# Attention heads grouped by the half in which their key/value head lies, and value products of 256 columns

## What is computed

```
q = q.reshape(bsz, nc, CHUNK, SWA_KV_HEADS, SWA_GROUP, SWA_HEAD_DIM) * SWA_HEAD_DIM ** -0.5
sc = jnp.einsum('bncvgd,bnkvd->bvgnck', q, k_band)
sc = sc + bias[None, :, :, None]
...
p = jnp.exp(sc - m)
p = p / (p.sum(-1, keepdims=True) + jnp.exp(sink - m))
o = jnp.einsum('bvgnck,bnkvd->bncvgd', p.astype(v_band.dtype), v_band)
o = o.reshape(bsz, s, SWA_WIDTH)
return (o * jax.nn.silu(gate)) @ w_out
```

## Time and profile before

| | |
|---|---|
| Median of 3 runs | 2330.74 us (2328.17 to 2332.15) |
| Profiled execution, its own time | 2325.54 us |
| Its span in the trace | 2323.7 us |
| PE busy | 2285.1 us, 98% |
| DVE, ACT, POOL busy | 75%, 50%, 15% |
| Chain that ended last | PE 78%, DVE 13%, issue 4%, DMA 3% |

### The profile page before, as it was taken

How to read it: one execution, slowest core, us unless ns; L and a number is a source line. 1 busy time by engine, 2 the same in 40 slices (tenths; PEclk the granted TensorE clock), 3 DMA queues, 4 the chain that set the end, 5 groups by cost and what they waited for, 6 DMA issues and landing times.

```text
span 2323.7 us, 30739 instructions
## 1 busy us (share of the span) xinstructions
PE 2285.1 (98%) x11554; PEld 1895.7 (82%) x11554; DVE 1753.4 (75%) x2442; ACT 1161.5 (50%) x1706; POOL 339.9 (15%) x340
## 2 busy tenths in 40 slices
PE   8999999999999999999999999999999999999997
PEld 6878878878888888887888888888888888888886
DVE  8788898875857669887696866897568667789448
ACT  4344455366435445536654544553655445554464
POOL 2311211122010111012201001110210110011031
PEclk9999999999999999999999999999999999999999
DMA  8787768654725435874484554585257345355324
GB/s 309 269 302 246 233 227 286 232 175 138 261 91 174 149 122 177 294 237 163 155 281 127 166 169 130 175 275 189 69 189 265 126 135 171 120 184 177 118 82 136
DMA packets 131043, 437.07 MB, mean 188 GB/s; under 512 B 13840, under 2 KB 18464, under 8 KB 130896
## 3 DMA queue, kind: packets, MB, share of 16 engines
q1 hardware_dynamic: 113232, 369.28, 48.4%
q0 software_dynamic: 17664, 65.83, 8.0%
HBM read 373.45 MB, written 57.41 MB: 185 GB/s over the span
## 4 chain that ended last, share of the span: by engine, by line
PE 78%; DVE 13%; issue 4%; DMA 3%; ACT 1%; POOL 1%; SPq 0%; POOLq 0%; DVEq 0%; ACTq 0%
PE accs L686 22%; PE accs L688 21%; PE accs L687 21%; DVE w_lo L1415 3%; PE bank L686 2%; PE bank L688 2%; PE bank L687 2%; PE bank L797 1%; PE bank L966 1%; PE bank L982 1%; PE bank L903 1%; PE bank L948 1%; DVE z L1759 1%; DMA stage<-w_qk 1%; DMA stage<-t_prep 1%
## 5 line engine op out<-in xcount | busy, mean ns | idle before, releaser
L1415 DVE TENSOR_TENSOR w_lo<-stage,w_hi 128x1024 fp32r<-128x1024 f32 x524 | 644.1, 1237 | 328.6 <-ACT w_hi L1057 327.5
L1057 ACT ACTIVATE w_hi<-stage 128x1024 fp32r<-128x1024 f32 x524 | 550.1, 1055 | 469.9 <-PE accs L688 179.6
L686 PE MATMUL accs<-w_hi,xs 128*128 128x512 f32 x1128 | 445.9, 395 | 7.9 <-ACT sg L1062 4.9
L688 PE MATMUL accs<-w_hi,xs 128*128 128x512 f32 x1128 | 439.8, 390 | 0.0
L687 PE MATMUL accs<-w_lo,xs 128*128 128x512 f32 x1128 | 439.3, 389 | 0.0
L686 PEld LDWEIGHTS accs<-w_hi,xs 128*128 128x128 f32 x1128 | 212.0, 188 | 54.4 <-issue 11.3
L688 PEld LDWEIGHTS accs<-w_hi,xs 128*128 128x128 f32 x1128 | 211.7, 188 | 45.0
L687 PEld LDWEIGHTS accs<-w_lo,xs 128*128 128x128 f32 x1128 | 212.0, 188 | 42.0
L686 PE MATMUL accs<-x_hi,w_hi 128*128 128x512 f32 (+1 forms) x640 | 244.2, 382 | 2.1 <-DVE qT L1860 1.5
L2134 POOL TENSOR_TENSOR rstd<-ve,half 128x1 f32<-128x1 f32 x96 | 81.6, 851 | 1124.5 <-DVE ve L1485 878.8
L688 PE MATMUL accs<-x_hi,w_lo 128*128 128x512 f32 (+1 forms) x640 | 236.5, 370 | 0.0
(11 more groups left out here) (213 smaller groups left out, 3780.9 us busy)
## 6 DMA issues: line engine op xcount, KB each, us to landing
stage<-t_prep SPq DMA_DIRECT2D x208, 512.0 KB, 3.7
stage<-w_vg SPq DMA_DIRECT2D x100, 512.0 KB, 3.6
stage<-w_qk SPq DMA_DIRECT2D x64, 512.0 KB, 3.5
stage<-w_swa SPq DMA_DIRECT2D x64, 512.0 KB, 4.0
t_prep<-t_buf POOLq DMA_DIRECT2D x28, 1024.0 KB, 5.3
stage<-w_ro SPq DMA_DIRECT2D x48, 512.0 KB, 3.5
cs<-rope_t SPq DMA_DIRECT2D x16, 1024.0 KB, 7.8
t_buf<-w_vg POOLq DMA_DIRECT2D x32, 512.0 KB, 9.2
```

Of the source, the lines that this page charges most:

```text
L686: mm(dst, lhs[0], rhs[0], start=start, stop=False, skip_group_check=reopened)
L688: return mm(dst, lhs[1], rhs[0], start=False, stop=stop, skip_group_check=reopened)
L1057: copy(w_hi[:, RING[g] % HS], stage[:, RING[g] % LS], ACT.Copy).then_inc(w_hi_made, 1)
L1415: nc.vector.tensor_tensor(w_lo[:, RING[g] % LS], stage[:, RING[g] % LS], w_hi[:, RING[g] % HS].bitcast(F32), sub).then_inc(w_split, 1)
```

## The change

Query heads are laid out anew, by the weights' order on the host: the two heads of a tile now belong to the two key/value heads of a pair, the lower one in partitions 0 to 63 and the upper one in 64 to 127, which is where the key product leaves their keys. `kT` becomes two tiles of two heads, each engine copies one bank of 128 partitions in one instruction, and the two key DMAs are gone. Bias, sinks and output weights follow the new order. The three `vs` DMAs move from slot KV + 6 to KV + 1 and wait there for `vt` alone. The first `score_pair` waits for the key copies; `kv_moved` (now 48 a block) is waited for by the first `weigh_pair`. With both heads of a key/value head side by side in `prT`, `weigh_pair` issues one product of 256 columns for two of 128.

```diff
-        kT = at("kT", [P, KVH, CHUNK + SB], X + 16 * KB)
+        kT = at("kT", [P, KVH // 2, CHUNK + SB], X + 16 * KB)
...
-                    if p == KV + 6:
-                        for m in range(4):
-                            sp.wait_ge(acc_free[m], emptied(s, KV, m))
-                        sp.wait_ge(carried, s + 1)
+                    if p == KV + 1:
+                        sp.wait_ge(y_free, emptied(s, KV, 3))
                         lo, hi = slice(0, CHUNK), slice(CHUNK, P)
-                        for src, dst, par in ((lo, hi, 0), (hi, lo, 1)):
-                            sp.dma_start(kT[dst, par:KVH:2, CHUNK:], kT[src, par:KVH:2, CHUNK:]).then_inc(kv_moved, 16)
                         sp.dma_start(vs[hi, :, :], vt[lo, :, :]).then_inc(kv_moved, 16)
                         sp.dma_start(vs[lo, 1:NT, :], vt[hi, 0:NT - 1, :]).then_inc(kv_moved, 16)
                         sp.dma_start(vs[lo, 0, :], vcar[hi, :]).then_inc(kv_moved, 16)
...
                 if j == 0:
-                    pe.wait_ge(kv_moved, 80 * (s + 1))
+                    pe.wait_ge(carried, s + 1)
+                    for m in range(2):
+                        pe.wait_ge(x_free, emptied(s, KV, m))
                     pe.wait_ge(x1_split, 8 * (s + 1))
...
-                    for i in range(4):
-                        kvh, e = 2 * g + i // 2, i % 2
-                        at_ = (2 * b + i // 2) * P
-                        mm = nc.tensor.matmul(bank[6][e * HD:(e + 1) * HD, at_:at_ + P],
-                                              val[:, kvh * HD:(kvh + 1) * HD], prT[:, u % 4, i * P:(i + 1) * P],
+                    for par in range(2):
+                        kvh = 2 * g + par
+                        mm = nc.tensor.matmul(bank[6][par * HD:(par + 1) * HD, 2 * b * P:2 * (b + 1) * P],
+                                              val[:, kvh * HD:(kvh + 1) * HD], prT[:, u % 4, 2 * par * P:2 * (par + 1) * P],
                                               start=True, stop=True)
...
-                        for e in range(2):
-                            rows = slice(e * HD, (e + 1) * HD)
-                            cp = copy(kT[rows, e, CHUNK:], acc[0][rows, :], ACT.Copy)
-                        cp.then_inc(acc_free[0], 1)
+                        copy(kT[:, 0, CHUNK:], acc[0], ACT.Copy).then_inc(acc_free[0], 1)
...
-                        for e in range(2):
-                            rows = slice(e * HD, (e + 1) * HD)
-                            cp = nc.vector.tensor_copy(kT[rows, 2 + e, CHUNK:], acc[1][rows, :])
-                        cp.then_inc(acc_free[1], 1)
+                        nc.vector.tensor_copy(kT[:, 1, CHUNK:], acc[1]).then_inc(acc_free[1], 1)
```

More of the change, by code:

```diff
@@ L335, in build @@
         mask = sb("mask", [P, P])
-        kcar = sb("kcar", [P, KVH, CHUNK])
+        kcar = sb("kcar", [P, KVH // 2, CHUNK])
         vcar = sb("vcar", [P, KVC])
@@ L457, in bias_band @@
         def bias_band(j, kvh):
-            off = (4 * kvh + 2 * j) * REP + CHUNK - 1
-            return bass.AP(bias_rep.tensor, off, [[NREL - 1, CHUNK], [REP, 2], [1, BAND]])
+            off = (4 * kvh + j) * REP + CHUNK - 1
+            return bass.AP(bias_rep.tensor, off, [[NREL - 1, CHUNK], [2 * REP, 2], [1, BAND]])
         def xbuf(s):
@@ L598, in _ @@
             for j in range(2):
-                sp.dma_start(sink[j * CHUNK:(j + 1) * CHUNK, :].rearrange("p (v e) -> p v e", e=2),
-                             bass.AP(a["swa_sinks"].tensor, 2 * j, [[0, CHUNK], [4, KVH], [1, 2]]))\
+                sp.dma_start(sink[j * CHUNK:(j + 1) * CHUNK, :],
+                             bass.AP(a["sinks"].tensor, 8 * j, [[0, CHUNK], [1, 8]]))\
                     .then_inc(const_loaded, 16)
@@ L962, in score_pair @@
                     for i in range(4):
-                        kvh, e = 2 * g + i // 2, i % 2
-                        rows = slice(e * HD, (e + 1) * HD)
[L965 to L968, removed]
+                        e, par = i // 2, i % 2
+                        rows = slice(par * HD, (par + 1) * HD)
+                        at_ = (2 * b + e) * BAND
+                        tiles = slice(4 * g + 2 * e, 4 * g + 2 * e + 2)
+                        mm = nc.tensor.matmul(bank[4 + 3 * par][:, at_:at_ + BAND],
+                                              qT[rows, c, tiles, :].rearrange("p a q -> p (a q)"),
+                                              kT[rows, g, c * CHUNK:c * CHUNK + BAND], start=True, stop=True)
                 mm.then_inc(s_full, 1)
             def weigh_pair(s, j):
+                if j == 0:
+                    pe.wait_ge(kv_moved, 48 * (s + 1))
                 pe.wait_ge(pT_copied, NU * s + 2 * j + 2)
@@ L1835, in softmax_front @@
                 need(dve, pT_full, NU * s + max(2 * j - 4, 0))
-                for e in range(2):
-                    ins = nc.vector.tensor_tensor(x[:, :, e:4:2, 0:BAND],
-                                                  bank[4 + 3 * e][:].rearrange("p (b i k) -> p b i k", b=2, i=2),
-                                                  bias[:, 4 * g + e:4 * g + 4:2, :].unsqueeze(1)
+                for par in range(2):
+                    ins = nc.vector.tensor_tensor(x[:, :, 2 * par:2 * par + 2, 0:BAND],
+                                                  bank[4 + 3 * par][:].rearrange("p (b i k) -> p b i k", b=2, i=2),
+                                                  bias[:, 4 * g + 2 * par:4 * g + 2 * par + 2, :].unsqueeze(1)
                                                   .to_broadcast([P, 2, 2, BAND]), add)
@@ L2011, in _ @@
                     if p == Q1 + 3:
-                        dve.wait_ge(kv_moved, 80 * (s + 1))
+                        dve.wait_ge(kv_moved, 48 * (s + 1))
+                        dve.wait_ge(x_free, emptied(s, KV, 0))
                         nc.vector.tensor_copy(kcar[:], kT[:, :, SB:SB + CHUNK])
@@ L2248, in weight_slots @@
     vg = w_in[:, 2 * D:].reshape(2, 2, 2, P, 2, RH, RV).transpose(5, 0, 4, 1, 3, 2, 6)
-    swa = w_swa.reshape(4, 2, P, 2, 2, 512).transpose(3, 4, 0, 2, 1, 5)
+    by_parity = w_swa.reshape(D, 2, 2, 2, 4, HD).transpose(0, 1, 2, 4, 3, 5)
+    swa = by_parity.reshape(4, 2, P, 2, 2, 512).transpose(3, 4, 0, 2, 1, 5)
+    w_sout = w_sout.reshape(2, 2, 4, HD, D).transpose(0, 2, 1, 3, 4).reshape(D, D)
     kv = w_kv.reshape(4, 2, P, 512).transpose(0, 2, 1, 3)
@@ L2258 @@
     x = np.asarray(x)
-    arrays = {"x_rows": x[0], "x_turned": x[0].T, "swa_sinks": swa_sinks, "rel_bias_table": rel_bias_table, "ln_gain": ln_gain, "ln_bias": ln_bias}
+    arrays = {"x_rows": x[0], "x_turned": x[0].T, "sinks": np.asarray(swa_sinks).reshape(8, 2).T, "rel_bias_table": rel_bias_table, "ln_gain": ln_gain, "ln_bias": ln_bias}
     arrays.update(weight_slots(*(np.asarray(w) for w in (ret_w_in[0], ret_w_out[0], swa_w_in[0], swa_w_out[0], swa_w_kv))))
```

## The result

The changed kernel is slower: 2340.09 us, the median of 6 runs (2337.42 to 2342.42), against 2331.44 for 6 runs of the kernel before on the same chip. The ratio is 1.0041, interval 1.0031 to 1.0052, so +9.6 us (7.2 to 12.1) by the ratio. The two medians lie 8.7 us apart. Forecast was 2330.4 with a range up to 2335.8. The profiled execution took 2337.42 us with a span of 2335.8 (before: 2325.54 and 2323.7).

The account below looks back on a forecast made before the run. TensorE was taken as the bound, busy 2285.1 us of 2323.7. Terms -0.4 (first scores), -0.5 (key banks), -0.3 (carried keys), -0.3 (value products) and +1.2 (shifts) sum to -0.3: median 2330.4 us, range 2326.3 to 2335.8.

Parts of the forecast that it names:

- How long will it take to land?: Q0 + 2's weight load behind the moved shifts: 6.9 to 4.8 us to land; 0.6 us stall in each of two blocks.
- 0.1 late: Q0 + 2 in the first block: lateness without the key moves' 1.3 us in the queue; 1.4 us with them.
- POOL's queue has no rows of this change: Remark closing the pricing of the shifts' move: POOL's queue is not edited; no time was put on it.
- Weights late for good: Rival at Q0 + 2: 9.7 us landings, stalls of 4.2 us in two blocks, 1.4 in two; 2340.4 us, chance 0.07.
- stands behind 512 KB at most: Argument against late weights: the 9.7 us load stood behind three weight loads, the Q0 + 2 load behind 512 KB at most.
- The row of 9.7 us: Profile row of the kernel before: one weight load behind the shifts took 9.7 us to land.
- the wait at the first scores: First `score_pair`, first block: PE's 0.40 us wait for the key DMAs goes, -0.4 us.
- the key banks: Third product group of Q0, third and fourth blocks: single key copies save 0.25 us each, -0.5 us.
- value products step as expected: `weigh_pair`: 256-column products run two at a time, 0.22 us apart; -0.01 us a pair, -0.3 us in all.
- the far bound of -2.7: Value products: if 0.17 us a pair were a cost per record, half would go, 0.085 x 32 = -2.7 us.
- the 6.4 of a fixed overhead a product: Value products: 60 cycles' overhead per matmul, read as an addition, gives 25 ns for each of 256 records, 6.4 us.
- the carried keys: DVE's copies ahead of `vt` and Q1's queries, halved to 128 columns: four times 0.07, -0.3 us, bounds 0 and -0.6.

Follow-up runs that it names:

- Experiment 1: The changed kernel with its three value shifts back at slot KV + 6 of SP's queue: 2329.21 us against 2330.71 for the kernel before, ratio 0.9995.
- experiment 5: The changed kernel with POOL's two late 512 KB loads held until PE has done Q0 + 1: 2330.24 us against 2329.91 for the kernel before, ratio 1.0005.

## Why the prediction was wrong, by its own steps

**The step that failed** is "How long will it take to land?". It took the landing of the loads that had stood behind the shifts at Q0 + 2, 6.9 us at most, with a discount of 1.3 for the key moves. Those rows came from a place where POOL's queue is silent; the new place is two microseconds behind 2 MB of POOL's, and SP's queue is empty when it gets there. It measured 9.9 us. The step took the loads' place in SP's own queue for the whole of what they wait behind. Against the likelier case of the text, "0.1 late", that is 4.3 us more, less 1.0 because SP reached the load sooner than priced (3.56 us after `vt` starts, not 4.6): 3.3 to 3.4 us late, as seen. The sentence "POOL's queue has no rows of this change" was true and beside the point: the order of a queue may stand still while its traffic decides.

**A term that was missing** is what a stall does behind itself. No sum, nor that of the rival, had the clock in it, which costs 1.6 us a stall and more, half as much again as the wait.

**"Weights late for good", at 0.07,** is what happened in kind, and its 2340.4 is 0.3 us from the result, but that closeness is luck. It had 4.2 us in each of the full blocks and 1.4 in each of the others; measured are 3.3 and 3.1 in the first two, 1.6 more in each for the clock, and nothing in the rest. What I held against it, that this load "stands behind 512 KB at most", counted SP's queue alone. The row of 9.7 us was the nearest one in kind and should have carried the weight: POOL had issued 2 MB there too, from 1021.86 to 1023.36 us, just ahead of that load's issue at 1024.0. Two slips of the working change nothing: the shifts moved by 16 us, not ten (461.26 to 446.47, in an execution that was 1.5 us later there), and half the spread of the three runs is 2.0 us, not 1.9.

**Right in the main:** the wait at the first scores went (-0.4); the key banks gave their quarter microsecond in the third and the fourth block; value products step as expected, two at a time, -0.01 us a pair, so neither the far bound of -2.7 nor the 6.4 of a fixed overhead a product came; the last two blocks hide the shifts, as forecast. Half right: the carried keys. PE's wait for `vt` fell from 0.20 to 0.08 us in the first block and to 0.13 in the second, as priced, but the waits for the queries stand at 1.5 as before, so the same copy on the way back gave nothing. Experiment 1 puts all of them together at -1.2 us, next to -1.5.

**The version to keep** is that of experiment 1: the change as it is, with the shifts where they stood. It is not measurably faster than the kernel before.

## What to carry to other kernels

When a DMA is moved ahead of loads, look up what every queue has in flight at the new place, not how long such loads took at the old one; the 2 MB that another engine had issued up to two microseconds earlier counted here in full. A wait put ahead of loads lets another engine's transfers come in ahead of them. Work on one scale (issue, landing, conversion, need, all from one event), and ask of each load how much of its lead it has left. A wait of several microseconds on TensorE can cost more than itself, since the products behind it ran at the lower clock for a while. And an early start for something that isn't wanted until 50 us later is no gain: at KV + 4 or KV + 6 the same DMAs were free.

## What the runs showed of the hardware

- A queue that had run empty waited behind the other's backlog: for 4.9 us after SP had issued its first shift, all packets moved were POOL's (2 MB issued). In experiment 5, with 1 MB, SP's first packets moved after some 2 us, and the same shift landed after 3.9 us, not 8.8. Where SP's queue was never empty the two shared: 348 packets of POOL's and 277 of SP's from 446 to 452 us in the kernel before.
- Shifts within SBUF and loads together moved few bytes for the engines' time. In experiment 5 SP's queue alone moved 239 GB/s at a share of 0.90 from 448.5 to 452 us, while the shifts ran, and 395 at 0.99 from 452 to 456 us, loads alone. POOL's store and loads had such a stretch too (246 GB/s at 0.97).
- Behind an idle time of 3.3 us the granted clock was 0.61 over 4 us, though it still read 1.00 in the last 2 us of idle time; some nine products went 0.43 us apart, 13 of them in one case. With PE busy there and the wait cut to 0.35 us it stayed at 1.00. The Trainium skill (TensorE: Matmul & The Clock Gate, Part 1) describes two levels, 1.2 GHz when idle and 2.4 when busy. The trace agrees: by these levels 512 columns take an estimated 0.427 and 0.213 us, and the products were 0.43 and 0.23 us apart.
- Issuing the three shifts held ACT's queue for 4.2 us and SP's for 2.3. What makes the difference was not tested.
